# Seven products instead of eight for most gate and up tile pairs of a feed-forward stage, with two of four weight sums made by accumulating transfers

## The reference

```python
h = rms_norm(x, norm_ffn_w[i])
g = jnp.einsum("bld,df->blf", h, w_gate[i])
u = jnp.einsum("bld,df->blf", h, w_up[i])
x = x + jnp.einsum("blf,fd->bld", jax.nn.silu(g) * u, w_down[i])
```

## Time and profile before

| | |
|---|---|
| median of 3 runs | 2689.13 us (2689.08 to 2689.93) |
| the profiled execution | 2689.1 us |
| its span | 2687.3 us |
| mean granted clock of TensorE, as a share of full speed | 0.996 |
| PE busy (matmuls) | 98% |
| VectorE (DVE) busy | 68% |
| ScalarE (ACT) busy | 48% |
| all transfers | 255.80 MB, 95 GB/s |

### The profile page before, as it was taken

How to read it: one execution, slowest core, us unless ns; L and a number is a source line. 1 busy time by engine, 2 the same in 40 slices (tenths; PEclk the granted TensorE clock), 3 DMA queues, 4 the chain that set the end, 5 groups by cost and what they waited for, 6 DMA issues and landing times.

```text
span 2687.3 us, 37446 instructions
## 1 busy us (share of the span) xinstructions
PE 2642.6 (98%) x15123; PEld 2235.7 (83%) x15123; DVE 1821.6 (68%) x2738; ACT 1285.0 (48%) x1956; POOL 26.7 (1%) x45
## 2 busy tenths in 40 slices
PE   9989999999999999999999999999999999999998
PEld 8777888988777888987889888888777888888996
DVE  7885746656885746666657556899978844674664
ACT  6784423336784423344323334445688453442332
POOL 0000000000000000000000000000000000000000
PEclk9999999999999999999999999999999999999999
DMA  6303233334203223232232242222222422223322
GB/s 217 94 2 110 95 90 107 94 90 163 79 2 110 102 86 110 95 106 82 83 114 95 90 158 79 72 78 71 78 92 90 133 95 94 94 92 91 116 84 74
DMA packets 80429, 255.80 MB, mean 95 GB/s; under 512 B 9600, under 2 KB 12800, under 8 KB 79872
## 3 DMA queue, kind: packets, MB, share of 16 engines
q1 hardware_dynamic: 77744, 240.29, 27.7%
q0 software_dynamic: 2512, 13.11, 1.4%
HBM read 241.30 MB, written 8.39 MB: 93 GB/s over the span
## 4 chain that ended last, share of the span: by engine, by line
PE 89%; DVE 6%; ACT 4%; issue 1%; DMA 0%; DVEq 0%; SPq 0%; ACTq 0%
PE PS L1607 22%; PE PS L1608 22%; PE PS L1609 22%; PE PS L1636 4%; PE PS L1638 4%; PE PS L1637 4%; PE PS L1886 1%; DVE WLO L2419 1%; PE PS L1868 1%; ACT WHI L1974 1%; PE PS L1566 1%; PE PS L1655 1%; PE PS L1654 1%; PE PS L1656 1%; PE PS L1832 0%
## 5 line engine op out<-in xcount | busy, mean ns | idle before, releaser
L2419 DVE TENSOR_TENSOR WLO<-WR,WHI 128x1024 fp32r<-128x1024 f32 (+4 forms) x482 | 518.6, 1080 | 402.8 <-ACT WHI L1974 400.4
L1974 ACT CAST WHI<-WR 128x1024 fp32r<-128x1024 f32 (+4 forms) x482 | 448.4, 931 | 525.4 <-PE PS L1609 410.9
L1607 PE MATMUL PS<-HHI,WHI 128*128 128x512 f32 x1680 | 670.4, 399 | 0.9 <-ACT Z L2086 0.9
L1609 PE MATMUL PS<-HHI,WLO 128*128 128x512 f32 x1680 | 654.9, 390 | 0.0
L1608 PE MATMUL PS<-HLO,WHI 128*128 128x512 f32 x1680 | 654.9, 390 | 0.0
L1607 PEld LDWEIGHTS PS<-HHI,WHI 128*128 128x128 f32 x1680 | 315.9, 188 | 70.6 <-issue 5.0
L1609 PEld LDWEIGHTS PS<-HHI,WLO 128*128 128x128 f32 x1680 | 315.5, 188 | 66.9
L1608 PEld LDWEIGHTS PS<-HLO,WHI 128*128 128x128 f32 x1680 | 316.0, 188 | 66.1 <-issue 4.4
L1607 PE MATMUL PS<-FHI,WHI 128*128 128x512 f32 x693 | 269.6, 389 | 0.0
L1608 PE MATMUL PS<-FLO,WHI 128*128 128x512 f32 x693 | 269.6, 389 | 0.0
L1609 PE MATMUL PS<-FHI,WLO 128*128 128x512 f32 x693 | 269.6, 389 | 0.0
(11 more groups left out here) (434 smaller groups left out, 4426.3 us busy)
## 6 DMA issues: line engine op xcount, KB each, us to landing
WR<-in_stream SPq DMA_DIRECT2D x338, 512.0 KB, 3.3
WR<-in_stream SPq DMA_DIRECT2D x64, 384.0 KB, 3.0
WR<-in_stream SPq DMA_DIRECT2D x64, 320.0 KB, 2.9
xkeep<-X POOLq DMA_DIRECT2D x3, 2048.0 KB, 9.1
X<-xkeep POOLq DMA_DIRECT2D x24, 256.0 KB, 5.6
WR<-in_stream SPq DMA_DIRECT2D x16, 328.0 KB, 4.3
ROT<-RQ SPq DMA_DIRECT2D x40, 64.0 KB, 2.0
X<-in_xin SPq DMA_DIRECT2D x8, 256.0 KB, 5.7
```

Source lines behind the costliest of these rows:

```text
L1607: e.matmul(out, hi[:, i, :], xhi, start=first, stop=False)
L1609: t = e.matmul(out, lo[:, i, :], xhi, start=False, stop=final)
L1974: e.copy(hi, raw).then_inc(S["act_high"], 1)
L2419: e.tensor_tensor(lo, raw, hi.bitcast(F32), ALU.subtract).then_inc(S["dve_low"], 1)
```

## The change

`SEVEN` becomes a tuple for each stage: pairs 5 to 21 (17 pairs) in stages 0, 1 and 3, and 8 to 21 (14 pairs) in the third, where before it was every second pair from 5 on (9 pairs) in all four. So pairs by seven products go from 36 to 65.

Two of the four weight sums leave VectorE. For each, SP issues a plain load of the upper half of the up block (`tget`), and when that has landed GpSimd issues a transfer that adds another half block out of HBM onto it (`tadd`, `accum_op=ALU.add`). Sum 0 of a pair (into TS: gate's upper half and up's upper half) feeds `tsum`, which now makes two sums from it. Sum 1 (into WS: both halves of up) is cast and split by itself (`thib`, `tlob`) into the unused half of the up slot. The up slot now loads and splits only its lower half. TS and TLO lie at the same address with two buffers, and so do WS and WLO; this sets what `tget` waits for: sum 0 of pair j for the second product (u = 1) of the pair two before, sum 1 for the end of the pair two before.

Products u = 1 and 2 trade places, the second `snap` goes within a bank of PSUM instead of into a tile, and `gs` and `cc` are one instruction each instead of two. The planner has a due time `ADDING = 3.0` for a sum by transfer, and an order of its own for the loads (`load_due`). Several semaphores are shared that were apart.

```diff
-SEVEN = range(5, FT, 2)
-PRODUCTS = ((0, 0, True), (1, 0, True), (2, 0, True), (0, 1, False), (0, 0, False), (1, 0, False), (2, 0, False))
+SEVEN = {f: tuple(range(5 if f != 2 else 8, FT)) for f in range(4)}
+PRODUCTS = ((0, 0, True), (2, 0, True), (1, 0, True), (0, 1, False), (0, 0, False), (1, 0, False), (2, 0, False))
...
+def two_before(f, j):
+    i = SEVEN[f].index(j)
+    return SEVEN[f][i - 2] if i >= 2 else None
...
     def load(self):
-        if self.next_load < len(self.slots):
+        self.due += 1
+        self.load_due()
+
+    def load_due(self):
+        while self.due and self.next_load < len(self.slots):
+            before = self.pair_of.get(self.next_load - RAW)
+            if before and not self.summed(before):
+                return
             self.add("load", self.next_load)
             self.next_load += 1
+            self.due -= 1
 
...
-        self.run(lambda: ("tlo", f, j, 1) in self.n)
         for u in range(7):
+            if u == 1:
+                self.run(lambda: ("tlo", f, j) in self.n)
+            elif u == 5:
+                self.run(lambda: ("tlob", f, j) in self.n)
...
-            if u == 0 or u == 2:
-                self.add("snap", f, j, u // 2)
-            elif u == 1:
+            if u == 0 or u == 1:
+                self.add("snap", f, j, u)
+            elif u == 2:
...
+        used = two_before(f, j)
+        if used is not None:
+            yield from self.added(("srow", f, used, 1, 3))
+            yield from self.until(("srow", f, used, 1, 3))
+        self.add("tget", f, j, 0)
+        yield self.add("tadd", f, j, 0)
+        self.spawn(self.last_sum(f, j, last))
+        yield ADDING
         while last - RAW not in self.low:
             yield 0.1
-        yield self.add("tsum", f, j)
+        if used is not None:
+            yield from self.added(("srow", f, used, 3, 3))
+            yield from self.until(("srow", f, used, 3, 3))
+        done = self.add("tsum", f, j)
+        self.load_due()
         self.advance()
-        if j - 2 in SEVEN:
-            yield from self.until(("srow", f, j - 2, 5, 3))
-        for k in range(2):
-            self.add("thi", f, j, k)
-        for k in range(2):
-            yield ("thi", f, j, k)
-            self.add("tlo", f, j, k)
+        yield done
+        yield self.add("thi", f, j)
+        self.add("tlo", f, j)
+
+    def last_sum(self, f, j, last):
+
+        while self.used + SPL <= last:
+            yield 0.1
+        self.add("tget", f, j, 1)
+        yield self.add("tadd", f, j, 1)
+        yield ADDING
+        yield self.add("thib", f, j)
+        self.add("tlob", f, j)
...
-    THI = sb("THI", 192, [4, T], F32R)
-    TLO = sb("TLO", 206, [4, T], F32R)
-    WT = sb("WT", 200, [2, T]), sb("WT2", 214, [2, T])
+    THI = sb("THI", 192, [2, 3, T], F32R)
+    TLO = sb("TLO", 206, [2, 3, T], F32R)
+    TS = sb("TS", 206, [2, 3, T])
+    WS = sb("WS", 48, [SPL, SLOT])
...
-                        q.wait_ge(S["dve_xlow"], n["tlo", f, j, 1])
+                        q.wait_ge(S["dve_xlow"], n["tlo", f, j])
                         q.wait_ge(S["dve_xlow"], n["sslo", f, 3])
                     elif u == 3:
                         q.wait_ge(S["act_uhi"], n["snap", f, j, 0])
                     elif u == 5:
+                        q.wait_ge(S["dve_xlow"], n["tlob", f, j])
                         q.wait_ge(S["dve_gs"], n["pd", f, j])
...
             elif kind == "thi":
-                f, j, k = a
+                f, j = a
+                total, hi, _ = sums(f, j)
                 q.wait_ge(S["dve_scale"], n["tsum", f, j])
-                if j - 2 in SEVEN:
-                    q.wait_ge(S["pe_prod"], o.product_end[f, j - 2, 5])
-                e.copy(THI[:, 2 * k:2 * k + 2, :].rearrange("p u c -> p (u c)"), WT[k][:, :, :].rearrange("p u c -> p (u c)")
-                       ).then_inc(S["act_xhigh"], 1)
+                e.copy(hi, total).then_inc(S["act_xhigh"], 1)
+            elif kind == "thib":
+                f, j = a
+                k = o.slot_of["seven", f, j][1]
+                added(q, f, j, 1)
+                e.copy(WHI[:, k % SPL, 0:T], WS[:, k % SPL, 0:T]).then_inc(S["act_xhigh"], 1)
             elif kind == "snap":
                 f, j, k = a
-                q.wait_ge(S["pe_prod"], o.product_end[f, j, 2 * k])
-                if j - 2 in SEVEN:
-                    q.wait_ge(S["dve_gs"], n["cc", f, j - 2])
-                e.copy((P1, Q5)[k][:, :], PS[o.bank["seven", f, j, 2 * k]][:, HALVES[0]]).then_inc(S["act_uhi"], 1)
+                q.wait_ge(S["pe_prod"], o.product_end[f, j, k])
+                if k == 0 and two_before(f, j) is not None:
+                    q.wait_ge(S["dve_gs"], n["ww", f, two_before(f, j)])
+                bank = PS[o.bank["seven", f, j, 2 * k]]
+                e.copy(bank[:, HALVES[1]] if k else first(f, j), bank[:, HALVES[0]]).then_inc(S["act_uhi"], 1)
...
-                q.wait_ge(S["dve_xlow"], n["tlo", f, j - 2, 1] if j - 2 in SEVEN else n["sslo", f, 3])
-                settle(e.tensor_tensor(WT[0][:, 0, :], gate[:, 0:T], up[:, 0:T], ALU.add))
-                e.tensor_tensor(WT[1][:, 0, :], up[:, 0:T], up[:, T:2 * T], ALU.add)
-                settle(e.tensor_tensor(WT[0][:, 1, :], WT[0][:, 0, :], up[:, T:2 * T], ALU.add))
-                e.tensor_tensor(WT[1][:, 1, :], WT[0][:, 1, :], gate[:, T:2 * T], ALU.add).then_inc(S["dve_scale"], 1)
+                used = two_before(f, j)
+                if used is None:
+                    q.wait_ge(S["dve_xlow"], n["sslo", f, 3])
+                else:
+                    q.wait_ge(S["pe_prod"], o.product_end[f, used, 3])
+                t1, t2, t4 = (TS[:, SEVEN[f].index(j) % 2, i, :] for i in range(3))
+                added(q, f, j, 0)
+                settle(e.tensor_tensor(t2, t1, up[:, T:2 * T], ALU.add))
+                e.tensor_tensor(t4, t2, gate[:, T:2 * T], ALU.add).then_inc(S["dve_scale"], 1)
             elif kind == "tlo":
-                f, j, k = a
-                q.wait_ge(S["act_xhigh"], n["thi", f, j, k])
-                e.tensor_tensor(TLO[:, 2 * k:2 * k + 2, :].rearrange("p u c -> p (u c)"), WT[k][:, :, :].rearrange("p u c -> p (u c)"),
-                                THI[:, 2 * k:2 * k + 2, :].rearrange("p u c -> p (u c)").bitcast(F32), ALU.subtract
-                                ).then_inc(S["dve_xlow"], 1)
+                f, j = a
+                total, hi, lo = sums(f, j)
+                q.wait_ge(S["act_xhigh"], n["thi", f, j])
+                e.tensor_tensor(lo, total, hi.bitcast(F32), ALU.subtract).then_inc(S["dve_xlow"], 1)
+            elif kind == "tlob":
+                f, j = a
+                k = o.slot_of["seven", f, j][1]
+                _, hi, lo = slot_tiles(k)
+                q.wait_ge(S["act_xhigh"], n["thib", f, j])
+                e.tensor_tensor(lo[:, 0:T], WS[:, k % SPL, 0:T], hi[:, 0:T].bitcast(F32), ALU.subtract).then_inc(S["dve_xlow"], 1)
...
             elif kind == "ww":
                 f, j = a
                 q.wait_ge(S["pe_prod"], o.product_end[f, j, 5])
-                settle(e.tensor_tensor(HF[:, j % 2, HALVES[1]], PS[o.bank["seven", f, j, 1]][:, HALVES[0]], P1[:, :], ALU.subtract))
+                settle(e.tensor_tensor(HF[:, j % 2, HALVES[1]], PS[o.bank["seven", f, j, 1]][:, HALVES[0]], first(f, j), ALU.subtract))
+                bank = PS[o.bank["seven", f, j, 0]]
+                e.tensor_tensor(bank[:, HALVES[1]], bank[:, HALVES[1]], HF[:, j % 2, HALVES[1]], ALU.subtract).then_inc(S["dve_gs"], 1)
+            elif kind == "gs" and a[1] in SEVEN[a[0]]:
+                f, j = a
+                rooted(q, NORM_FFN[f])
+                q.wait_ge(S["dve_gs"], n["ww", f, j])
                 if j >= 2:
                     q.wait_ge(S["dve_mul"], n["mul", f, j - 2])
-                e.tensor_tensor(SQ[:, j % 2, HALVES[1]], PS[o.bank["seven", f, j, 0]][:, HALVES[1]], HF[:, j % 2, HALVES[1]],
-                                ALU.subtract                                ).then_inc(S["dve_gs"], 1)
-            elif kind == "gs" and a[1] in SEVEN:
-                f, j = a
-                rooted(q, NORM_FFN[f])
-                q.wait_ge(S["pe_slot"], o.slot_of["seven", f, j][0] + 1)
-                e.tensor_tensor(SQ[:, j % 2, HALVES[0]], PS[o.bank["seven", f, j, 0]][:, HALVES[0]], RS[:, HALVES[0]], ALU.mult)
-                q.wait_ge(S["dve_gs"], n["ww", f, j])
-                e.tensor_tensor(SQ[:, j % 2, HALVES[1]], SQ[:, j % 2, HALVES[1]], RS[:, HALVES[1]], ALU.mult).then_inc(S["dve_gs"], 1)
+                e.tensor_tensor(SQ[:, j % 2, :], PS[o.bank["seven", f, j, 0]][:, :], RS[:, :], ALU.mult).then_inc(S["dve_gs"], 1)
             elif kind == "cc":
                 f, j = a
                 q.wait_ge(S["act_uhi"], n["snap", f, j, 1])
-                q.wait_ge(S["dve_gs"], n["gs", f, j])
-                e.tensor_tensor(HF[:, j % 2, HALVES[1]], HF[:, j % 2, HALVES[1]], Q5[:, :], ALU.add)
```

(21 more changed lines are left out.)

104 lines of the change are left out of this document (63 added, 41 removed).

## The result

The changed kernel takes 2989.74 us (median of 4 runs, 2986.65 to 2993.17); the kernel before, run beside it, 2689.40 (4 runs). The ratio is 1.1117, 95% interval 1.1098 to 1.1136: 300 us slower, where the prediction had 75 and its range ended at 2850. The direction was right, the size off fourfold. The profiled execution took 2991.7 us.

What follows compares the result with a forecast made beforehand. TensorE, busy 98% of the span, was taken as the bound. -24.4 - 11.4 + 79.0 + 31.4 = +74.6 us on 2689.1 gave 2764 us; likeliest range 2735 to 2810, range over all 2684 to 2850.

Steps and rivals of the forecast that it cites:

- Matmuls, -24.4: On TensorE, 65 pairs by seven products instead of 36 remove 24.4 us of matmuls.
- the third stage, -11.4: Third stage's pairs 5 and 7 become pairs by eight, so their lost time of 11.4 us goes.
- The waits, 79.0 + 31.4 = 110.4: TensorE's added waiting for late sums: 79.0 us in later pairs of the stages, 31.4 at the stages' first pairs.
- VectorE's loop, 10.50 us: VectorE's list for one seven pair takes 10.50 us against TensorE's 10.07, holding it back 0.43 us a pair.
- First pair of a stage, 9.9 + 9.9 + 7.6 = 27.4 us, 31.4 with the clock: Pair 5's sums come late: TensorE waits 9.9 us at u = 1 in stages one and two, 7.6 at u = 3 in the fourth.
- The transfers, 2.77 + 3.5 and hand-overs = 6.73 us: Sum 0 is there 6.73 us after u = 1: fetch 2.77, addition 3.5, the rest matmul end and hand-overs.
- Circle A: From u = 3 through u = 1, sum 0's transfers and back to u = 3: 22.84 us for two pairs, 11.42 each.
- Rival 2: The addition is as slow as queued transfers, 5.6 us: some 2880 us; 0.17 together with rival 3 above 2810.
- Both leave 1.4 us of waiting in a pair: Circle A (11.42 us) and a circle through sum 1 (11.45 us) each exceed TensorE's 10.07 us pair by 1.4.
- The sums of 11 and 12 are made under the down products and cost nothing: Sums for pairs 11 and 12 cost nothing; if that cover failed, some 6.5 us a stage.
- rival 3: TensorE's lower clock after waits: +12 us, 2776, or towards 2840; 0.17 together with Rival 2 above 2810.
- The +34 us by it: Forecast sum if fetch and addition took the skill's 2.6 us each, 5.2 in place of 6.3: +34 us.

Runs made afterwards that it cites:

- number 8: The kernel before, with the third stage's seven pairs beginning at pair 9 in place of 5, still every second pair; 2677.83 us, ratio 0.9961.
- number 1: The changed kernel with GpSimd's adding transfers left out, readers of the sums waiting for the plain fetches; 2707.5 us.
- Number 13: The changed kernel with every other pair by seven, from pair 7 (third stage from 9), and ADDING = 9.0; 2680.78 us, ratio 0.9971.
- number 3: The changed kernel with 24 matmuls of 256 columns, their result overwritten, added ahead of u = 2 of each seven pair; 3012.5 us.
- number 7: The changed kernel with every other pair by seven (34 in all, third stage from 9), transfers kept, ADDING = 3.0; 2918.7 us, ratio 1.086.
- alternating kernel: The changed kernel with every other pair by seven (34 in all), transfers kept; 2918.7 us with ADDING = 3.0, 2695.48 us with 9.0.
- number 10: The changed kernel with every other pair by seven (34 in all), transfers kept, ADDING = 9.0; 2695.48 us, ratio 1.0023.
- number 14: The changed kernel with two of three pairs by seven, from pair 8 (third stage 9), 39 pairs, ADDING = 9.0; 2693.0 us, ratio 1.0015.

## Why the prediction was right in direction and wrong in size

- **Matmuls, -24.4, and the third stage, -11.4:** right. 16167 matmuls as forecast, and number 8 shows the third stage's term by itself: -11.4 in all where -9.7 was forecast.
- **The waits, 79.0 + 31.4 = 110.4:** wrong by a factor of three. In the PE timeline the 65 pairs by seven last 337 us more than at 10.07 each; less 35.8 that is 302, the difference of the two profiled spans to 1 us. The next points share it out.
- **VectorE's loop, 10.50 us:** right, 10.46 to 10.47 in number 1. This alone leaves "all pairs by seven" next to no gain over "every other".
- **First pair of a stage, 9.9 + 9.9 + 7.6 = 27.4 us, 31.4 with the clock:** the mechanism is right, the size near: the waits at u = 1 are 11.97, 11.62 and 4.92 us, and the three pairs last 24.62, 24.25 and 21.15, which is 39.8 over 10.07. The fourth stage's stands mostly at u = 1 and not at u = 3; the prediction's own list had tlo late there too. Number 13 (those stages from pair 7) is free of such waits.
- **The transfers, 2.77 + 3.5 and hand-overs = 6.73 us:** this step failed first. The medians are 3.8 + 5.1, so with the same hand-overs 9.36, and in the pair shown it was 10.46. I had taken the addition "nearer to the lonely one" of the bounds 3.0 and 5.6, "since these too come one at a time", and they don't: in the pair shown both leave GpSimd 0.63 us apart. Circle A needs this once in two pairs, so its 11.42 us become 12.7 to 13.3, and the forecast some 2850 to 2890 (an estimate: half of the 2.6 to 3.7 us in 41 pairs, all of it in seven first ones and in six sums at the starts). That is 90 to 125 of the 226 us that were missing. Rival 2, the slow addition at 2880, named this part and was given too little.
- **"Both leave 1.4 us of waiting in a pair":** this step failed with it, and for a second reason. I had followed sum 0 through its data only, and not through SP's list: 18 waits of SP for TensorE ahead of a fetch, where circle A supposes one in nearly every pair. The 16 pairs named above, whose fetch had stood behind weight loads, hold 114 us of the miss. Where circle A binds, as in the pair shown, the lower clock adds 1.5 us in two pairs.
- **"The sums of 11 and 12 are made under the down products and cost nothing":** right for both sums 0, whose tsum are made at 446.02 and 455.71 in the first stage, ahead of pair 11 (463.28). Sum 1 of pair 11 was late by 2.7 us of TensorE's time there. The 20 to 22 us of pair 12 are for sum 0 of pair 13, whose fetch stood in SP's list.
- **The clock:** rival 3 had it as a cost of up to 76 us. It shows, as 97 us of slow matmuls, but with number 3 most of the clock came back and no time. It costs where no other wait of like length stands beside it (2.1 us a pair in number 7).
- **What the prediction lacked altogether** is a question to the order: where does the first reader of a slow transfer stand, and who is queued behind it? I had read that tsum stands ahead of ww and gs, but used it only to follow a circle, with each engine's wait as a link of it. But a reader placed too early stalls its engine even where no circle exists: 223 us in the alternating kernel from this one number, and 125 in the full change. The planner's 3.0 was in the diff, against the prediction's own 6.73 for the same way.

Weighed against the Trainium skill ("DMA: Bandwidth & Descriptors", Anatomy of one DMA), its 2.0 us and bytes at 436 GB/s, 2.6 us for 256 KB as an estimate, are given for transfers that GpSimd issues. The plain fetches, which SP issues, took 2.6 us (sum 1 in number 10) to 3.8 by the median; the additions, which GpSimd issues and which its figures do not cover, 3.8 to 5.3. The +34 us by it was farther off than the sum's +74.6. The profile's own spread, 3.0 to 5.6 for one shape and queue, was the better guide for the additions.

What stays open: why neighbouring seven pairs in a list of two of three still take up to 13.7 us, which number 14's view of PE's waits spreads over VectorE's pd (6.2 us) and ScalarE's copies (9.7); and how fast the full change would be with thi placed ahead of the silu and a sum that lands in time. It needs an order that the planner's one number can't give, and it wasn't tried. VectorE's 10.46 us a pair alone would give 2689.1 - 35.8 + 57 x 0.39, some 2676 us (an estimate), so it would be a gain of 13 at best; number 1, without additions but with the order for 3.0, took 2707.5. Nor was the full change at 3.0 run with sum 0's fetch in a queue where nothing stands ahead of it or behind it, so how the loss splits between transfers and SP's list is worked out here and not measured.
